# RMS norm between the stages of a decoder layer: token sums broadcast by a product with ones, with root and reciprocal taken of 512 columns in every partition

## What is computed

```
def rms_norm(x, g):
    y = x * lax.rsqrt(jnp.mean(x * x, axis=-1, keepdims=True) + EPS)
    return y * g
...
h = modulate(rms_norm(x, g_ffn1[i]), sh1, sc1)     # norm 0
x = x + 0.5 * (1.0 + gt1) * swiglu(h, w1_ffn1[i], w3_ffn1[i], w2_ffn1[i])
h = modulate(rms_norm(x, g_mix[i]), sh2, sc2)      # norm 1
...
h = modulate(rms_norm(x, g_ffn2[i]), sh3, sc3)     # norm 2
x = x + 0.5 * (1.0 + gt3) * swiglu(h, w1_ffn2[i], w3_ffn2[i], w2_ffn2[i])
return rms_norm(x, g_final)                        # norm 3
```

## Time and profile before

| | us |
|---|---|
| median of 3 runs | 1172.69 |
| lowest and highest | 1172.61, 1173.48 |
| the profiled execution's own time | 1173.75 |
| its span | 1172.0 |
| TensorE busy in it | 1141.2 |
| VectorE busy | 542.6 |
| ScalarE busy | 485.2 |

### The profile page before, as it was taken

The page is one execution under the profiler, slowest core; times in us unless marked ns, Lnnn a source line. Parts: engine busy times, 40 slices in busy tenths (PEclk is TensorE's granted clock), DMA queues, the critical chain, the costliest instruction groups (busy, mean ns, idle before and its releaser), DMA issues.

```text
span 1172.0 us, 14826 instructions
## 1 busy us (share of the span) xinstructions
PE 1141.2 (97%) x5467; PEld 909.2 (78%) x5467; DVE 542.6 (46%) x890; ACT 485.2 (41%) x856; POOL 158.6 (14%) x98
## 2 busy tenths in 40 slices
PE   5999999999999999999999999999999999999996
PEld 4688888888888878676777778887888888888885
DVE  3544444444344354489785546545333333332321
ACT  4455655556444232134555555334232232232223
POOL 0135454454433210000000000000000000000000
PEclk9999999999999999999999999999999999999998
DMA  9845655655555342222222113322242242233211
GB/s 309 267 144 182 223 168 179 209 185 172 169 170 170 89 117 73 54 55 72 55 55 55 55 55 90 90 72 72 72 137 77 77 138 72 90 130 99 99 50 72
DMA packets 159098, 138.23 MB, mean 118 GB/s; under 512 B 3551, under 2 KB 157522, under 8 KB 159058
## 3 DMA queue, kind: packets, MB, share of 16 engines
q1 hardware_dynamic: 130948, 109.38, 30.2%
q10 hardware_dynamic: 28110, 28.32, 7.5%
HBM read 135.59 MB, written 2.10 MB: 117 GB/s over the span
## 4 chain that ended last, share of the span: by engine, by line
PE 90%; DVE 6%; ACT 1%; issue 0%; ACTq 0%; POOLq 0%; POOL 0%; DVEq 0%
PE ps L352 27%; PE ps L354 27%; PE ps L353 27%; PE ps L970 2%; PE ps L945 2%; PE ps L955 2%; DVE score L1302 1%; PE ps L383 1%; DVE max L1300 1%; PE ps L893 1%; DVE h_lo L439 1%; DVE w_lo L331 1%; PE ps L800 1%; DVE nrm L433 1%; PE ps L481 1%; DVE score L1290 0%
## 5 line engine op out<-in xcount | busy, mean ns | idle before, releaser
L331 DVE TENSOR_TENSOR w_lo<-raw,w_hi 128x1024 fp32r<-128x1024 f32 (+1 forms) x164 | 239.4, 1460 | 419.5 <-ACT w_hi L326 419.5
L352 PE MATMUL ps<-h_hi,w_hi 128*128 128x512 f32 x1024 | 407.2, 398 | 5.3 <-DVE h_lo L439 5.0
L354 PE MATMUL ps<-h_hi,w_lo 128*128 128x512 f32 x1024 | 400.1, 391 | 0.0
L353 PE MATMUL ps<-h_lo,w_hi 128*128 128x512 f32 x1024 | 399.7, 390 | 0.0
L326 ACT ACTIVATE w_hi<-raw 128x1024 fp32r<-128x1024 f32 (+1 forms) x164 | 183.2, 1118 | 266.4 <-PE ps L354 266.2
L352 PEld LDWEIGHTS ps<-h_hi,w_hi 128*128 128x128 f32 x1024 | 192.8, 188 | 53.5 <-issue 8.7
L354 PEld LDWEIGHTS ps<-h_hi,w_lo 128*128 128x128 f32 x1024 | 192.6, 188 | 41.1
L353 PEld LDWEIGHTS ps<-h_lo,w_hi 128*128 128x128 f32 x1024 | 192.8, 188 | 38.0 <-issue 0.5
L352 PE MATMUL ps<-g_hi,w_hi 128*128 128x512 f32 x352 | 138.4, 393 | 0.2 <-DVE w_lo L331 0.2
L354 PE MATMUL ps<-g_hi,w_lo 128*128 128x512 f32 x352 | 137.2, 390 | 0.0
L353 PE MATMUL ps<-g_lo,w_hi 128*128 128x512 f32 x352 | 137.1, 389 | 0.0
(11 more groups left out here) (166 smaller groups left out, 873.8 us busy)
## 6 DMA issues: line engine op xcount, KB each, us to landing
raw<-in_w_ffn SPq DMA_DIRECT2D x42, 1024.0 KB, 5.4
ada<-in_w_ada ACTq DMA_DIRECT2D x27, 1024.0 KB, 5.1
raw<-in_w_ffn SPq DMA_DIRECT2D x16, 1408.0 KB, 6.3
raw<-in_w_in SPq DMA_DIRECT2D x64, 256.0 KB, 3.2
ada<-in_w_ada SPq DMA_DIRECT2D x16, 512.0 KB, 8.7
raw<-in_w_out SPq DMA_DIRECT2D x16, 256.0 KB, 3.0
x_tok<-in_x SPq DMA_DIRECT2D x4, 512.0 KB, 5.4
raw<-in_w_ffn SPq DMA_DIRECT2D x8, 256.0 KB, 7.3
```

What stands on the lines that cost most here:

```text
L331: nc.vector.tensor_tensor(tiles_of(w_lo[j % SPL], nk), raw_of(f, j, nk), tiles_of(w_hi[j % SPL], nk).bitcast(F32), ALU.subtract).then_inc( ...
L352: nc.tensor.matmul(ps[:, bank, :], hi, rhs_hi, start=start, stop=False)
L353: nc.tensor.matmul(ps[:, bank, :], hi, rhs_lo, start=False, stop=False)
L354: return nc.tensor.matmul(ps[:, bank, :], lo, rhs_hi, start=False, stop=stop)
```

## The change

For norms 1 and 2 the sums of all tokens come from two products with a 128 x 128 matrix of ones as one operand and 512 columns of squares as the other, which leaves each token's mean square in all 128 partitions of the bank: `tmp[:, 2]` first, then, when tile 7 is squared, the last square. ScalarE takes the root of the whole bank into `tmp[:, 3]`, VectorE the reciprocal of that in place, and `nrm` reads it there instead of from PSUM. The diagonal matrices and the product that broadcast them go. The factor 1/1024 moves from the root into the squares (for norm 3 too). The Silu table is brought in right after the root instead of after the last `h_hi`. Norm 0 keeps its way, its code written out in place.

```
         def act_square(act, n, k):
...
-            nc.scalar.activation(tmp[:, k % 2, :], xT[:, k, :], ACT.Square).then_inc(sq_done, 1)
+            nc.scalar.activation(tmp[:, k % 2, :], xT[:, k, :], ACT.Square, scale=D_MODEL ** -0.5).then_inc(sq_done, 1)
...
-        def pe_sum(pe, n):
-
-            if n:
-                pe_keep_busy(8)
-                pe_token_sums(pe, n)
-                pe_keep_busy(6)
-            pe.wait_ge(diag_done, n + 1)
-            nc.tensor.matmul(ps[:, B_SUM, :], ones[:, :], tmp[:, 3, :], start=True, stop=True).then_inc(row_done, 1)
-            if n:
-                pe_keep_busy(10)
+        def pe_bcast_sum(pe, n):
+
+            pe.wait_ge(acc_done, 6 * n)
+            nc.tensor.matmul(ps[:, B_SUM, :], ones[:, :], tmp[:, 2, :], start=True, stop=False)
+            pe_keep_busy(4)
+            pe.wait_ge(sq_done, KD * n)
+            nc.tensor.matmul(ps[:, B_SUM, :], ones[:, :], tmp[:, (KD - 1) % 2, :], start=False, stop=True).then_inc(sum_done, 1)
+            pe_keep_busy(12)
...
         def dve_scaled(n, k):
 
-            nc.vector.scalar_tensor_tensor(nrm[:, k % 4, :], ps[:, B_SUM, :], a_mul[:, n, k:k + 1], xT[:, k, :],
+            nc.vector.scalar_tensor_tensor(nrm[:, k % 4, :], tmp[:, 3, :] if n else ps[:, B_SUM, :], a_mul[:, n, k:k + 1], xT[:, k, :],
                                            ALU.mult, ALU.mult).then_inc(u_done, 1)
...
         def dve_h(dve, n):
-            dve_rstd(dve, n)
-            dve.wait_ge(row_done, n + 1)
+            dve.wait_ge(sqrt_done, n + 1)
+            nc.vector.reciprocal(tmp[:, 3, :], tmp[:, 3, :]).then_inc(rstd_done, 1)
+            dve.wait_ge(rstd_done, n + 1 + (2 if n == 2 else 0))
             dve_scaled(n, 0)
...
         def act_h(act, n):
-            act_sqrt(act, n)
+            act.wait_ge(sum_done, n)
+            nc.scalar.activation(tmp[:, 3, :], ps[:, B_SUM, :], ACT.Sqrt, bias=eps[:, :]).then_inc(sqrt_done, 1)
+            if n == 2:
+                act_warm(act, ACT.Silu)
             for k in range(KD):
                 act.wait_ge(u_done, KD * n + k + 1)
                 nc.scalar.activation(h_hi[:, k, :], nrm[:, k % 4, :], ACT.Identity,
                                      bias=mods[:, 24 * n + k:24 * n + k + 1]).then_inc(hhi_done, 1)
-            if n == 2:
-                act_warm(act, ACT.Silu)
```

More of the change, by code:

```diff
@@ L409, in act_warm @@
             nc.scalar.activation(warm[:, :], eps[:, :], func)
[L411 to L418, removed]
         def dve_diag(dve, dst, r, done_sem, count):
@@ L425, in dve_diag @@
                                     r.unsqueeze(2).broadcast_to([P, QT, P]), ALU.mult).then_inc(done_sem, 1)
-        def dve_rstd(dve, n):
-            dve.wait_ge(sqrt_done, n + 1)
-            dve_diag(dve, tmp[:, 3, :], rtok[:, :], diag_done, n + 1 + (2 if n > 1 else 0))
         def dve_scaled(n, k):
-            nc.vector.scalar_tensor_tensor(nrm[:, k % 4, :], ps[:, B_SUM, :], a_mul[:, n, k:k + 1], xT[:, k, :],
+            nc.vector.scalar_tensor_tensor(nrm[:, k % 4, :], tmp[:, 3, :] if n else ps[:, B_SUM, :], a_mul[:, n, k:k + 1], xT[:, k, :],
                                            ALU.mult, ALU.mult).then_inc(u_done, 1)
@@ L833, in _ @@
             pe.wait_ge(x_done, KD)
-            pe_sum(pe, 0)
+            pe.wait_ge(diag_done, 1)
+            nc.tensor.matmul(ps[:, B_SUM, :], ones[:, :], tmp[:, 3, :], start=True, stop=True).then_inc(row_done, 1)
             row_sums(0)
@@ L841, in _ @@
             pe_ffn(pe, 0)
-            pe_sum(pe, 1)
+            pe_bcast_sum(pe, 1)
             def single(u):
@@ L1008, in _ @@
                 unit(OUT_BANK[q % 4], q, h_hi, h_lo).then_inc(unit_done, 1)
-            pe_sum(pe, 2)
+            pe_bcast_sum(pe, 2)
             pe_ffn(pe, 1)
@@ L1029, in _ @@
                                      accum_out=tsum[:, t:t + 1]).then_inc(tok_sum, 1)
-            act_sqrt(act, 0)
+            act.wait_ge(tok_sum, QT)
+            nc.scalar.activation(rtok[:, :], tsum[:, :], ACT.Sqrt, bias=eps[:, :], scale=1.0 / D_MODEL).then_inc(sqrt_done, 1)
             for k in range(0, KD, 2):
@@ L1165, in _ @@
             act.wait_ge(sum_done, 3)
-            nc.scalar.activation(rtok[:, :], ps[:, B_SUM, 0:QT], ACT.Sqrt, bias=eps[:, :], scale=1.0 / D_MODEL)\
-                .then_inc(sqrt_done, 1)
+            nc.scalar.activation(rtok[:, :], ps[:, B_SUM, 0:QT], ACT.Sqrt, bias=eps[:, :]).then_inc(sqrt_done, 1)
             act_token_major(act, KD - 1)
@@ L1191, in _ @@
                 if k == 5:
-                    dve_rstd(dve, 0)
+                    dve.wait_ge(sqrt_done, 1)
+                    dve_diag(dve, tmp[:, 3, :], rtok[:, :], diag_done, 1)
                 dve.wait_ge(xt_psum, k + 1)
```

## The result

| | before | changed |
|---|---|---|
| median, 15 runs each, us | 1173.48 | 1175.66 |
| lowest to highest | 1172.03 to 1175.20 | 1172.87 to 1177.73 |
| profiled execution: time, span | 1173.75, 1172.0 | 1175.99, 1174.3 |
| ratio to before | | 1.0017, 95% interval 1.0011 to 1.0024 |

The change makes the kernel slower: by 2.18 us between the medians, by 2.0 us (1.3 to 2.8) by the ratio, which is worked out from the single runs. The forecast was +3.9 us, 1176.6 us from a median before of 1172.69.

The account below looks back on a forecast made before the run. Bound taken: the serial path between stages at norms 1 and 2. Each transition: reciprocal 4.24 - 2.28 = +1.96 us, two +3.92, from the 1172.69 median to 1176.6 us; range 1172.5 to 1180.0.

Parts of the forecast that it names:

- The sign and the size: Whole kernel: slower, +1.96 us at each of two transitions, +3.92 us in all; slower was given 0.68.
- the break-even: Norms 1 and 2: the change gains only if the wide reciprocal takes under 2.28 us, 4.1 ns an element.
- The path and its steps: Norms 1 and 2: one serial path from last square to TensorE's next useful product, 8.65 us between stages; steps count twice.
- The floor under the reciprocal: VectorE, norms 1 and 2: split w_lo holds the reciprocal until 409.34 at norm 1, so it starts only 0.19 us earlier.
- The price of the reciprocal: VectorE, 512 columns at norms 1 and 2: 8.0 ns per further element, 4.24 us; span 0.48 to 4.24.
- the prediction's own formula: Each transition changes by R + 0.03 - 2.12 - 0.19 = R - 2.28 us, R being the 512-element reciprocal's time.
- The Trainium skill's rule: VectorE's divide repeats 8 times; taken as cycles, 8.3 ns an element, a 4.4 us reciprocal, +4.2 us in all.
- The other reading: VectorE's divide as a pipeline across eight slices taking an element each cycle, the mechanism for a fast reciprocal.
- Rival (a): Norms 1 and 2: reciprocal streams like other operations, 0.69 us, -3.2 us in all, 1169.5 us; chance 0.20.
- Rival (b): Norms 1 and 2: in-between pace such as 5.5 ns, reciprocal 2.96 us, +1.36 us in all, 1174.1 us; chance 0.12.
- Rival (c): After both transitions: slow reciprocal plus TensorE's clock falling while idle, up to 3.4 us more, 1180.0 us; chance 0.08.
- The other edits at nothing: Norms 1 and 2: nrm from SBUF, the factor in the squares, the moved Silu table and unread products cost nothing.

Follow-up runs that it names:

- The three kernels above: The kernel before with four sum products ahead of the last-square wait, with the last w_lo split behind the diagonals, or with both: ratios 0.9985, 1.0001, 0.9971.
- early sums alone: The kernel before with four of the eight sum products ahead of the wait for the last square, norm 3 too: 1170.87 us, ratio 0.9985.
- the moved split alone: The kernel before with each transition's last w_lo split moved on VectorE from ahead of the reciprocal to behind the diagonals: 1173.36 us, ratio 1.0001.
- both together: The kernel before with the sums ahead of the wait, the split behind the diagonals and six unread products instead of nine: 1169.52 us, ratio 0.9971.

## Why the prediction was right, point by point

- **The sign and the size.** The sign was well founded: both slopes that the prediction read, 5.5 and 8.0 ns, lie above the 4.1 of the break-even. The size was not: +3.9 us was forecast and +2.18 measured, and that is one term, the price of the reciprocal (below). The median of 1175.66 lies in the forecast's own range of 1175.2 to 1178, but by luck: that range was counted from a median before of 1172.69, so it stands for +2.5 to +5.3 us, and +2.18 is just under it.
- **The path and its steps.** Right. Both transitions moved by the same amount, TensorE's first product moved with them, and every step stood where it was put: the second product 407.32, 0.06 us after the square ended (0.15 was foreseen); the root 0.69 us (up to 0.72); the hand-over on VectorE 412.76 - 409.38 - 3.35 = 0.03.
- **The floor under the reciprocal.** Right in kind, 0.09 us off in size. I took the split's end for the start of the reciprocal, 0.19 us sooner than before, and said that the split hides up to 0.2 us of the root; it was 0.17. It starts 0.09 us ahead of the listed end of the split, so 0.28 us sooner. The three kernels above show the floor directly, in the kernel before.
- **The price of the reciprocal.** The mis-sized term. "I take 8.0" ns for each element, 4.24 us in all; it measured 6.25 ns and 3.35 us. The method was right (the same operation at two widths), but the choice of 8.0 over 5.5 had too little under it: the difference of two means over two elements holds no more than the span of 5.5 to 8.0 that the same rows gave. The truth lay inside it, 0.75 above the low figure and 1.75 below the one that I took. With R = 3.35 the prediction's own formula gives 3.35 - 2.28 = +1.07 a transition, and +0.98 with the 0.09 above. Measured is +0.99 and +0.98. The sum, +1.97 us, is within the interval of the +2.18 us that the runs show.
- **The Trainium skill's rule** ("VectorE: DVE Perf Modes", section "First, the fixed hardware budget", a repeat count of 8) pointed the right way, but the estimate of 8.3 ns that was worked out from it is a third too high; 6.25 ns is six cycles at the 0.96 GHz of that page. The other reading (the Trainium skill, "Vector Engine (DVE) Microarchitecture Reference", section "3.2 Anatomy of a single slice", taken as an element a cycle) is out: the line through 2, 128, 256 and 512 columns leaves no room for it.
- **Rival (a)** lost on its mechanism, and was right on its price: it had -3.2 to -3.6 us, and with the plain scaling of 0.42 us the two transitions give 2 x -1.94 = -3.88. The 169 ns of a scaling of 4 elements against 170 to 175 of the reciprocal, which spoke for it, compared operations with different fixed parts: 169 ns at 4 elements and 420 at 512 put the scaling's at an estimated 167 ns, and the reciprocal's is 147.
- **Rival (b)** was nearer in size than the forecast: +1.4 us for 5.5 ns and +3.9 for 8.0, with +2.18 measured. At 0.17% the result also lies inside the band of 0.2% to which I had given 0.12, though 15 runs each tell it from no change.
- **Rival (c)** happened in its first half: the clock did fall after both transitions. No cost of it shows: the kernel with thirty unread products kept the clock up and took as long behind norm 1 (372.01 us both); behind norm 2 it took 366.04 us, between the 366.01 and 366.31 of the profiles with a fallen clock. The reason was the one given, VectorE's pace.
- **The other edits at nothing.** Right: `nrm` from SBUF takes as long as from PSUM (1.41 for the pair in both), the table shows no cost in either place, the square with a factor takes 0.63 as before.

## What to carry to other kernels

A wide elementwise step in the place of a narrow one plus a broadcast is a matter of one price, so measure that price before anything else: the break-even (here 2.28 us) can be worked out from the profile of before, and then a single instruction decides. At 0.147 us and 6.25 ns for each element the break-even of 2.28 us is an estimated 340 columns. Keep a divide on the narrow side of a broadcast. When an engine becomes free sooner, look at what stands ahead of the next step in the queue of the engine that takes it: early sums alone won 0.28 us a transition, the moved split alone nothing, both together 0.96.

## What the runs showed of the hardware that I had not expected

- VectorE's reciprocal of float32 takes 6.25 ns for each element of a partition and 0.147 us besides, at 128, 256 and 512 elements. Other operations of 512 columns in these traces take 0.42 to 0.86 us on average.
- A stretch of 4.1 us without TensorE was followed by half clock for most of 3.8 us at norm 1 and for all of 5.5 us at norm 2, at no cost that shows, as the first tiles came no faster than half clock could take them. The fall of the clock after the one-column products near 450 does cost. The kernel with the narrower reciprocals is the only one whose profiled execution has none; this is the stretch of its windows that stands beside the 0.63 of the earlier trace rows:

```profile
453.40:456.80 3.40, 3.40 (x17) 2.79 (x16) 0.48 (x6) 0.00 (x0) 0.00 (x0) 1.00 0.51 149
```

From the first product behind norm 1 to the last square of norm 2 it took 370.4 us, where the others took 371.9 to 372.0. That is 1.5 us, within the up to 1.7 that the prediction put on one fall. It is one execution, and why it escaped the fall I did not try. Such a difference, which no edit here aims at, is as large as the effects that these experiments measure, so the distances in the traces carry more weight than the times.
